# The last k-steps ahead of a norm by token halves, the norm's rsqrt by columns, part of the scaling on GpSimd, and 18 idle matmuls in place of 28

## The reference

```python
# first block
y, yc = neighbourhood_attention(h, hc, w_qkv, q_g, k_g, rpb, w_o, ...)
x = x + g1 * y                                             # residual after w_o
hf = modulate(rms_norm(x, norm_ffn_g), sh2, sc2)           # norm "f"
x = x + g2 * conv_ffn(hf, w_up, conv_w, conv_b, w_down)    # residual after w_down
# second block
h = rms_norm_2(x, norm_g)                                  # norm "h"
proj = jnp.einsum('bsd,dn->bsn', h, w_in)
...
return x + jnp.einsum('bsd,de->bse', y, w_out)             # last product
```

## Time and profile before

| | us |
|---|---|
| median of 3 runs | 2547.7 |
| lowest and highest run | 2546.64, 2549.43 |
| span of the profiled execution | 2544.7 |
| PE busy | 2512.1 (99%) |
| PE, weight loads | 2130.9 (84%) |
| DVE busy | 1621.3 (64%) |
| ACT busy | 1250.3 (49%) |
| POOL busy | 144.6 (6%) |
| mean granted clock of PE | 0.998 of full speed |

### The profile page before, as it was taken

The page is one execution under the profiler, slowest core; times in us unless marked ns, Lnnn a source line. Parts: engine busy times, 40 slices in busy tenths (PEclk is TensorE's granted clock), DMA queues, the critical chain, the costliest instruction groups (busy, mean ns, idle before and its releaser), DMA issues.

```text
span 2544.7 us, 34507 instructions
## 1 busy us (share of the span) xinstructions
PE 2512.1 (99%) x13608; PEld 2130.9 (84%) x13608; DVE 1621.3 (64%) x2365; ACT 1250.3 (49%) x1897; POOL 144.6 (6%) x148
## 2 busy tenths in 40 slices
PE   6999999999999999999999999999999999999999
PEld 2688899998888888888888898988888888888887
DVE  3567787886588886566665666665555554545554
ACT  3244433334465554355554555555566665544443
POOL 1001100000001110001110000001000000000000
PEclk9999999999999999999999999999999999999999
DMA  9953777775569885566665465556554555555555
GB/s 335 340 182 113 239 244 241 244 248 183 208 192 274 265 257 195 193 189 189 191 189 190 163 178 174 174 166 186 172 163 150 160 169 186 182 190 186 187 189 165
DMA packets 459104, 511.42 MB, mean 201 GB/s; under 512 B 36771, under 2 KB 327682, under 8 KB 458432
## 3 DMA queue, kind: packets, MB, share of 16 engines
q1 hardware_dynamic: 455936, 501.11, 62.1%
q0 software_dynamic: 2864, 8.11, 1.1%
q10 hardware_dynamic: 144, 0.02, 0.0%
HBM read 506.93 MB, written 2.22 MB: 200 GB/s over the span
## 4 chain that ended last, share of the span: by engine, by line
PE 94%; ACT 2%; DVE 1%; SPq 1%; issue 1%; DMA 1%; DVEq 0%; ACTq 0%
PE PG L925 17%; PE PG L927 17%; PE PG L926 17%; PE PG L915 13%; PE PG L918 6%; PE PG L934 4%; PE PG L936 4%; PE PG L935 4%; PE PS L1039 1%; PE PS L830 1%; SPq L745 1%; PE PG L846 1%; PE PS L1103 1%; ACT wh L1178 1%; PE PG L848 1%
## 5 line engine op out<-in xcount | busy, mean ns | idle before, releaser
L1573 DVE TENSOR_TENSOR wl<-raw,wh 128x1024 fp32r<-128x1024 f32 (+1 forms) x745 | 911.2, 1227 | 699.2 <-ACT wh L1178 697.4
L1178 ACT ACTIVATE wh<-raw 128x1024 fp32r<-128x1024 f32 (+1 forms) x745 | 786.2, 1057 | 863.5 <-PE PG L927 575.6
L915 PE MATMUL PG<-FHL,wh 128*128 128x512 f32 x1376 | 430.7, 396 | 2.4 <-DVE UP L1829 1.5
L925 PE MATMUL PG<-wh,HHL 128*128 128x512 f32 x832 | 331.2, 398 | 0.1
L927 PE MATMUL PG<-wl,HHL 128*128 128x512 f32 x832 | 324.8, 390 | 0.0
L926 PE MATMUL PG<-wh,HHL 128*128 128x512 f32 x832 | 324.1, 390 | 0.0
L918 PEld LDWEIGHTS PG<-FHL,wl 128*128 128x128 f32 x1376 | 256.2, 188 | 59.6
L918 PE MATMUL PG<-FHL,wl 128*128 128x256 f32 x1376 | 267.9, 278 | 0.0
L915 PEld LDWEIGHTS PG<-FHL,wh 128*128 128x128 f32 x1376 | 210.8, 189 | 5.2 <-issue 3.7
L927 PEld LDWEIGHTS PG<-wl,HHL 128*128 128x128 f32 x832 | 156.2, 188 | 33.6
L926 PEld LDWEIGHTS PG<-wh,HHL 128*128 128x128 f32 x832 | 156.5, 188 | 30.6
(11 more groups left out here) (402 smaller groups left out, 4216.4 us busy)
## 6 DMA issues: line engine op xcount, KB each, us to landing
raw<-in_w_in SPq DMA_DIRECT2D x208, 512.0 KB, 3.4
raw<-in_w_up SPq DMA_DIRECT2D x344, 256.0 KB, 3.4
raw<-in_w_ada SPq DMA_DIRECT2D x128, 512.0 KB, 5.1
raw<-in_w_down SPq DMA_DIRECT2D x84, 512.0 KB, 4.0
raw<-in_w_qkv SPq DMA_DIRECT2D x80, 512.0 KB, 4.6
first<-in_w_ada SPq DMA_DIRECT2D x78, 256.0 KB, 6.8
raw<-in_w_o SPq DMA_DIRECT2D x32, 512.0 KB, 3.7
raw<-in_w_in SPq DMA_DIRECT2D x64, 256.0 KB, 3.0
```

Of the source, the lines that this page charges most:

```text
L915: pe.matmul(to, hi[:, 128 * j:128 * j + 128], flat(FHL[:, step.k, :, :]), start=step.first, stop=False, skip_group_check=True)
L925: pe.matmul(dst, xh[:, cols], hi, start=step.first and j % per == 0, stop=False, skip_group_check=True)
L1178: ac.activation(wh[n % NSPL][:, 0:src.shape[1]], src, ACT.Copy).then_inc(S["hi"], 1)
L1573: dv.tensor_tensor(wl[n % NSPL][:, 0:x], src, wh[n % NSPL][:, 0:x], ALU.subtract).then_inc(S["lo"], 1)
```

## The change

Four things are changed.

- In group 3 of `wo`, `down1` and `wout`, the k-steps of the last two tiles (four; in `down1` three) run token half by token half: all of them for half 0, then all for half 1. A semaphore `half` is raised when half 0 is complete. `used` for a tile is raised once half 1 is through with it. `res` (for every group) and `out` handle half 0 first, multiply and then add, with the wait for half 0 only, then half 1.
- The norm's rsqrt has a form of its own, with two columns handled apart: each round is a multiply of two per-partition scalars and a multiply-add, for column 0 and for column 1. The function `rsqrt` loses its parameter `to`.
- For norm "f", chunks 3 to 7 of half 0 are scaled on POOL in place of ACT.
- `warm` has 18 matmuls in place of 28, at both norms.

```diff
+        w.wait_ge(S["xr"], nth("norm", "f", 0))
+        for i in range(3, 8):
+            po.tensor_scalar(HN["f"][:, 0, T * i:T * i + T], XT[:, 0, T * i:T * i + T], xr[:, 0:1], None,
+                             ALU.mult).then_inc(S["scaled_p"], 1)
         for g in range(43):
...
+            if name in HALVES and g == 3 and step.k >= nk - 2 - tiles[-1][3]:
+                by_halves(step)
+                return
...
+        def by_halves(step):
+            name, g, k0, nk, tiles = P.prods[step.p]
+            ps = result(name, g)
+            first = nk - 2 - tiles[-1][3]
+            units = [(j, k) for j in range(2) for k in range(first, nk)]
+            n = 2 * (step.k - first)
+            for j, k in units[n:n + 2]:
+                m = P.tile0[step.p] + k // 2
+                c = k % 2
+                w.wait_ge(S["lo"], m + 1)
+                xh, xl = operands(name, k)
+                hi, lo = (x[m % NSPL][:, 512 * c:512 * c + 512] for x in (wh, wl))
+                cols = slice(128 * j, 128 * j + 128)
+                pe.matmul(ps[:, j, :], xh[:, cols], hi, start=False, stop=False, skip_group_check=True)
+                pe.matmul(ps[:, j, :], xl[:, cols], hi, start=False, stop=False, skip_group_check=True)
+                end = pe.matmul(ps[:, j, :], xh[:, cols], lo, start=False, stop=k == nk - 1, skip_group_check=True)
+                if j == 0 and k == nk - 1:
+                    end.then_inc(S["half"], 1)
+                if j == 1 and (c == 1 or k == nk - 1):
+                    end.then_inc(S["used"], 1)
...
-                for n in range(28):
+                for n in range(18):
...
             elif job == "scale":
                 z, i = key
+                if pooled(z, i):
+                    return
...
             elif job == "norm":
                 n = nth("norm", key, 0)
+                v, y, a, h = (CV[:, i, 0:2] for i in range(4))
                 w.wait_ge(S["xsq"], 4 * n)
                 w.wait_ge(c.sem, c.n)
-                dv.scalar_tensor_tensor(out=xss[:, :], in0=xsq[:, :, 3], scalar=1.0 / D, in1=xss[:, :], op0=ALU.mult,
+                dv.scalar_tensor_tensor(out=v, in0=xsq[:, :, 3], scalar=1.0 / D, in1=xss[:, :], op0=ALU.mult,
                                         op1=ALU.add).then_inc(c.sem, c.up())
-                rsqrt(xss[:, :], 2, 0.0, to=(xr[:, :], S["xr"], n))
+                w.wait_ge(c.sem, c.n)
+                dv.tensor_scalar(h, v, -0.5, -0.5e38, ALU.mult, ALU.max).then_inc(c.sem, c.up())
+                dv.tensor_scalar(y.bitcast(I32), v.bitcast(I32), -0.5, 1597463007.0, ALU.mult,
+                                 ALU.add).then_inc(c.sem, c.up())
+                for i in range(3):
+                    done = c.n
+                    for j in range(2):
+                        w.wait_ge(c.sem, done if i == 0 else done - 1 + j)
+                        dv.tensor_scalar(a[:, j:j + 1], y[:, j:j + 1], y[:, j:j + 1], h[:, j:j + 1], ALU.mult,
+                                         ALU.mult).then_inc(c.sem, c.up())
+                    for j in range(2):
+                        w.wait_ge(c.sem, done + 1 + j)
+                        end = dv.scalar_tensor_tensor(out=(xr if i == 2 else y)[:, j:j + 1], in0=a[:, j:j + 1], scalar=1.5,
+                                                      in1=y[:, j:j + 1], op0=ALU.add, op1=ALU.mult)
...
-                w.wait_ge(*product_done(name, g))
...
-                dv.tensor_tensor(RTMP[:, 0, :], result(name, g)[:, 0, :], gate, ALU.mult).then_inc(c.sem, c.up())
-                dv.tensor_tensor(RTMP[:, 1, :], result(name, g)[:, 1, :], gate, ALU.mult).then_inc(out_sem(name, g), 1)
                 for j in range(2):
-                    w.wait_ge(*((c.sem, c.n) if j == 0 else out_done(name, g)))
+                    w.wait_ge(*half_done(name, g, j))
+                    end = dv.tensor_tensor(RTMP[:, j, :], result(name, g)[:, j, :], gate, ALU.mult)
...
                     dv.tensor_tensor(x[:, j, :], RTMP[:, j, :], x[:, j, :], ALU.add).then_inc(S["res"], 1)
...
             elif job == "out":
                 g = key
-                w.wait_ge(*product_done("wout", g))
                 w.wait_ge(S["res"], 24)
                 for j in range(2):
+                    w.wait_ge(*half_done("wout", g, j))
```

More of the change, by code:

```diff
@@ L48 @@
 UP_PASS = ((0, 22, 0, 22), (22, 43, 22, 21))
+HALVES = ("wo", "down1", "wout")
 class Waits:
@@ L439 @@
         "qn_sq", "kn_sq", "q_tok", "k_tok", "l_max", "l_exp", "l_sum", "gated", "ha_hi", "ob_hi",
-        "mv_ones", "grow", "zeros", "y_part", "y", "y_hi", "xo")
+        "mv_ones", "grow", "zeros", "y_part", "y", "y_hi", "xo", "half", "scaled_p")
 def build(nc, I, out):
@@ L510, in build @@
     lsum = const("lsum", [128, 4])
-    CV = const("CV", [128, 3, 8])
+    CV = const("CV", [128, 4, 8])
     CSs = const("CSs", [128, 2, KC])
@@ L651, in q_result, with half_done @@
         return result("q", g)[:, 0, :]
+    def half_done(name, g, j):
+        if j == 0 and g == 3 and name in HALVES:
+            return S["half"], HALVES.index(name) + 1
+        return product_done(name, g)
     def product_done(name, g):
@@ L669, in mod_done, with pooled, scaled @@
         return S["mod_lo"], nth("mod", (z, c), 1)
+    def pooled(z, i):
+        return z == "f" and i >= 3
+    def scaled(z, i, n):
+        if n == 0 and pooled(z, i):
+            return S["scaled_p"], i - 2
+        before = 0 if z == "f" else (3, 8)[n]
+        return S[f"scaled{n}"], before + i + 1
     def gate_cols(name, g):
@@ L1090, in piece @@
                     for n in range(2):
-                        w.wait_ge(S[f"scaled{n}"], nth("scale", (name[1], i), 0))
+                        w.wait_ge(*scaled(name[1], i, n))
                 else:
@@ L1574, in split_upto, with rsqrt @@
                 front[0] += 1
-        def rsqrt(src, n, eps, sem=None, mean=1, to=None):
+        def rsqrt(src, n, eps, sem=None, mean=1):
             v, y, a = CV[:, 0, 0:n], CV[:, 1, 0:n], CV[:, 2, 0:n]
@@ L1599, in rsqrt @@
                 w.wait_ge(c.sem, c.n)
[L1600 to L1604, removed]
                 dv.scalar_tensor_tensor(out=y, in0=a, scalar=1.5, in1=y, op0=ALU.add,
@@ L1688, in piece @@
                 n = nth("norm", key, 0)
+                v, y, a, h = (CV[:, i, 0:2] for i in range(4))
                 w.wait_ge(S["xsq"], 4 * n)
                 w.wait_ge(c.sem, c.n)
-                dv.scalar_tensor_tensor(out=xss[:, :], in0=xsq[:, :, 3], scalar=1.0 / D, in1=xss[:, :], op0=ALU.mult,
+                dv.scalar_tensor_tensor(out=v, in0=xsq[:, :, 3], scalar=1.0 / D, in1=xss[:, :], op0=ALU.mult,
                                         op1=ALU.add).then_inc(c.sem, c.up())
-                rsqrt(xss[:, :], 2, 0.0, to=(xr[:, :], S["xr"], n))
+                w.wait_ge(c.sem, c.n)
[12 more added lines that the diff above has]
+                                                      in1=y[:, j:j + 1], op0=ALU.add, op1=ALU.mult)
+                        if i < 2:
+                            end.then_inc(c.sem, c.up())
+                        elif j == 1:
+                            end.then_inc(S["xr"], 1)
             elif job == "presum":
@@ L1820, in piece @@
                 w.wait_ge(S["res"], 2 * n)
-                dv.tensor_tensor(RTMP[:, 0, :], result(name, g)[:, 0, :], gate, ALU.mult).then_inc(c.sem, c.up())
-                dv.tensor_tensor(RTMP[:, 1, :], result(name, g)[:, 1, :], gate, ALU.mult).then_inc(out_sem(name, g), 1)
                 for j in range(2):
-                    w.wait_ge(*((c.sem, c.n) if j == 0 else out_done(name, g)))
+                    w.wait_ge(*half_done(name, g, j))
+                    end = dv.tensor_tensor(RTMP[:, j, :], result(name, g)[:, j, :], gate, ALU.mult)
+                    if j == 0:
+                        end.then_inc(c.sem, c.up())
+                        w.wait_ge(c.sem, c.n)
+                    else:
+                        end.then_inc(out_sem(name, g), 1)
+                        w.wait_ge(*out_done(name, g))
                     dv.tensor_tensor(x[:, j, :], RTMP[:, j, :], x[:, j, :], ALU.add).then_inc(S["res"], 1)
```

## The result

| | before | after |
|---|---|---|
| median | 2547.5 us | 2553.9 us |
| lowest and highest | 2546.6, 2549.4 | 2551.7, 2555.4 |
| ratio of the medians, 95% interval | | 1.0024 [1.0015, 1.0034] |
| executions | 8 | 8 |
| span of the profiled execution | 2544.7 us | 2553.6 us |

The change makes the kernel slower by 0.24%, 6.4 us. The forecast was 2552.0 us, and the range, to 2554.6, holds the result; of the rivals the nearest is the one called full price (2554.3).

The account below looks back on a forecast made before the run. PE was taken as full nearly everywhere, so only its pauses count. From 2547.7 us, first norm +2.5, second +0.6, last product -0.6 (sum +2.5) and clock +1.8 gave 2552.0 us, range 2548.8 to 2554.6.

Parts of the forecast that it names:

- full price: Rival, chance 0.24: half clock wholly on PE-bound steps after each norm, GpSimd blocks DVE's first subtract; 2554.3 us.
- The new stall: Last `wo` product: PE waits about 1.4 us for tile 7's subtract, product ends at 712.04 in place of 710.64.
- The later release: Both norms: first gate multiply queued behind a weight subtract delayed by later tile release; +2.33 us first, +0.68 second.
- Residual and squares: Both norms: first multiply to first norm step takes 3.50 us in place of 3.29, +0.21 us each.
- The rsqrt by columns: Both norms: norm steps take 2.05 us in place of 2.36, -0.3 us each, between -0.6 and 0.
- GpSimd: First norm: its five scalings may collide with DVE's work ahead of the first matmul, +0.3 us, from 0 to +1.0.
- The end: Last product: the first half's add lies under the matmuls, -0.6 us, bounds 0 and -1.0.
- The clock: Both norms: 18 idle matmuls leave PE gaps of 3.0 and 3.7 us, clock falls to half; +1.8 us, 0.9 each.
- The likeliest outcome by sign: Whole kernel: difference within 0.2% (5.1 us), chance 0.65; slower by more 0.32, faster by more 0.03.
- The rival in which the change does what it seems made for: Chance 0.08: half 0's residual is over when the product ends at both norms; -4.3 us, 2543.4 us.

Follow-up runs that it names:

- halves alone: Kernel before with only the last tiles, `res` and `out` by token halves (28 idle matmuls, old rsqrt, no GpSimd scaling): 2551.7 us, 1.0015.

## Why the prediction was right, and where not

The sum can be set against stretches of PE's time in single traces, with after_28 meaning after with 28 idle matmuls:

| stretch | before | after_28 | difference | forecast |
|---|---|---|---|---|
| `wo` from its start to its end | 98.7 | 100.8 | +2.1 | +1.4 |
| end of `wo` to the end of `down1` | 729.6 | 731.3 | +1.7 | +1.1 |
| end of `down1` to the end of `wout` | 1100.6 | 1101.4 | +0.8 | +0.6 |
| end of `wout` to the span's end | 3.9 | 3.2 | -0.7 | -0.6 |
| sum | | | +3.9 | +2.5 |

The medians give +3.9 too. Point by point:

- *The new stall*: right. The trace gives 1.29 us of idle time, 1.4 forecast, for the subtract it named. By the starts of the matmuls it costs 1.6: in the trace of after_28 the one behind the stall starts 1.68 us after the one ahead, and the next 0.34 after that, in place of 0.227 each.
- *The later release*: right, in cause and size. The product ended at 713.70 and the multiply stands 1.13 us after it (714.83), forecast 1.14; the halves gained nothing, since they were queued behind the subtract. The versions with the subtract moved are the only ones faster than before. They differ from after in more than that (old residual order elsewhere, 22 idle matmuls, no GpSimd part), but with those out a loss of some 2.8 us is left (an estimate: 3.9 less the 1.1 of the residual, below), and with the subtract moved half 0's multiply starts 2.4 us before the product's end. That shows this cause, not only its signs.
- *Residual and squares*: right at the norms, 3.53 us from the first multiply to the norm (714.83 to 718.36), forecast 3.50. But wrong in reach: this is the step that failed. The diff says "for every group", and I worked it out for group 2 of `wo` and group 3 alone. At each other group the same 0.25 us delays ACT's next copy, and PE has no slack there. It costs 0.2 us in each of groups 1 and 2 of `wo`, and of the 1.7 in the second line only 1.1 lies between the product's end and the next product's first matmul (9.90 us against 8.80), which leaves 0.6. About +1.1 in all, taken at nothing. The kernel before with the new order alone shows the same: `wo` 99.3 us against 98.7, in three groups, and 1.0 us more to the end of `down1`, 0.3 of it at the norm. Both experiments on it point the same way in their medians (-1.0 and +1.8 us), each with an interval wider than the effect, so its size rests on the traces. The rest of the 1.4 us by which the sum fell short is 0.2 of the stall and 0.2 of the rsqrt at the second norm, less 0.1 at the end.
- *The rsqrt by columns*: the direction right, the size not. 2.27 us (718.36 to 720.63) in place of 2.36, so -0.1, not -0.3 and far from -0.6. The pair of multiplies with two pointers each takes 0.45 us, the pair of multiply-adds without a pointer 0.28, and a round 0.56 where I took 0.50.
- *GpSimd*: +0.3 taken, nothing measured, the lower bound. It sits beside DVE's scalings, ahead of nothing that is late: from the first scaling to the first matmul of `up` pass 2.97 us with it (after_28) and 2.95 without (halves alone). At the first norm this error and that of the rsqrt, -0.3 and +0.2, nearly cancel; that is luck.
- *The end*: right, -0.7.
- *The clock*: right that it falls at both gaps, which measure 3.25 and 3.93 us (3.0 and 3.7 forecast). Its price is 2.1 to 2.5 us of medians, 1.8 forecast. The profiled execution of after pays more, about 4.0: end of `wo` to end of `down1` 732.9 us against 731.3, and from there to the end of `wout` 1103.8 against 1101.4. Its half-clock stretches are the long ones, some 7 us. The other executions of after range over 3.7 us, which would fit a mixture of long and short ones; their clocks by stretch aren't recorded, and their mean clocks (0.995 to 0.998) don't settle it, so that isn't shown.

The likeliest outcome by sign, within 0.2% with 0.65, did not come by the median, though the interval reaches below 0.2%. The missed residual term alone doesn't explain it: 1.1 us less would be 2552.8 (+5.3), and the run with the old order where no norm follows is 5.2 us above its kernel before. The rival nearest in time, full price, was near for other reasons than its own: GpSimd cost nothing, and the clock less than 3.4 by the medians. The rival in which the change does what it seems made for needed further edits, the subtract's place above all, but also the old residual order elsewhere, group 2's pieces at k-step 4 and 22 idle matmuls, and then came out at 2544.1 where it had named 2543.4.

## What to carry over

To have work ready early helps only if nothing waits ahead of it in its engine's queue: before splitting a result in two so that a follower can start sooner, read what stands between the follower and its place in program order, and which buffer release that waits for. When a diff changes a helper, price it at every place that calls it, and where PE has no slack even 0.25 us on a feeding engine comes out on PE. Idle matmuls that bridge a chain are sized to the chain: shorten the chain first, then cut them.

## What was not expected of the hardware

- The clock fell after a gap of only 2.17 us followed by 12 transposes (before with 18), and held after gaps of 1.67 and 1.76 us followed by the same transposes (after with 28, halves alone). The Trainium skill (TensorE: Matmul & The Clock Gate, "Part 4: PE-mode transpose") says that transposes don't count as busy in the way of matmuls; the 2.17 us case is in line with it, and nothing here shows it alone. In after the clock fell 2.1 us into the first gap, ahead of any transpose, so there the gap alone did it.
- The stretch at half clock was about 3.5 us at four norms (both of before with 18; the first of after without GpSimd and of after with the old residual order) and about 7 at four (both of after, the second of the other two). At the first norm three kernels had the same gap of 3.25 us, and one of them a long stretch. Windows of half a microsecond show what goes with it: in the four long ones the clock fell 0.9 to 1.6 us before the transposes started, in the four short ones at most 0.1 us before them or up to 0.9 us after. Why it falls sooner in one trace than in another isn't shown.
- Three DVE scalings of 128x256 took 1.30 us beside GpSimd's and 0.88 without them. GpSimd's own took 0.96 us each, one engine's row of after:

```profile
720.70 4.79 POOL L805 TENSOR_SCALAR HNF<-XT,xr 128x256 f32<-128x256 f32 x5 [3.90 <-DVE xr L1748]
```

- Scalars by pointer seem to cost more than the width on tiny steps: two 128x1 multiplies with two pointers each took 0.45 us, two 128x1 multiply-adds without 0.28. The operations differ too; with two columns and no pointer they took 0.17 and 0.16 us.
